# Down products of a feed-forward stage: one 128-row accumulation, or two 64-row accumulations in two PSUM banks

## Chip, cores and metric

The kernel runs on one core of a Trainium2 chip. The metric is device time in microseconds (us) of one execution of the program, the median of several. TensorE (PE in the profile, with its weight loads as PEld) multiplies, VectorE is DVE, ScalarE is ACT, GpSimd is POOL, SyncE is SP, and SP's DMA queue is SPq.

## What is computed

Two decoder layers over 288 token columns (256 of a prompt, 8 x 4 of samples). Each layer mixes by three branches (a recurrent one, windowed attention, pooling) and ends with the feed-forward part that the change touches:

```python
h = rmsnorm(x, norm_ffn) @ w_up                 # 1024 -> 4096
x = x + jnp.square(jax.nn.relu(h)) @ w_down     # 4096 -> 1024
```

All arrays are float32.

## The kernel before

**Layout.** Features lie on partitions, tokens along the free axis: `x` is 8 tiles of 128 x 288. Weights come in units of 128 x 1024 (eight 128 x 128 blocks) into a ring of four slots (`RING`), three units ahead (`LEAD`). Each unit is split into two reduced-precision halves: ACT copies it to `w_hi` (L720), DVE subtracts to get `w_lo` (L949). Activations are split likewise (`a_hi`, `a_lo` in front of the up products; `h_hi`, `h_lo` in front of the down products). A product of one 128 x 128 block is then three matmuls, hi x hi, hi x lo and lo x hi, each with a weight load of its own, so a unit is 8 x 3 = 24 matmuls of 128 rows, 128 output columns and 288 moving columns into one PSUM bank (`product`, L402). The four banks `PZ` take the units in turn. The four banks `PM` serve attention, norms and the recurrent state, and stand unused in the turns that the change touches.

**The feed-forward turns.** It is cut into `FI` = 4 turns of 16 units in each layer (`ffn_turn`, L671): units j = 0 to 7 are up products, each giving one of the eight tiles of h; units j = 8 to 15 are down products, each of which reads all eight tiles of h (k = 0 to 7) and gives one tile of x.

**Order of the work.** Each engine runs a list written by hand, and semaphores order the engines. In one turn, for an up unit, DVE waits for `unit_done`, takes relu times rstd out of PSUM (L1270), ACT squares it (L880) and copies it to `h_hi` (L882), DVE subtracts to get `h_lo` (L1274) and counts up `f_lo`. PE reads h with one wait for each k in unit 8 alone:

```python
have = (lambda k: pe.wait_ge(s["f_lo"], l * 8 * FI + i * 8 + (k + 1) + HEAD)) if j == 8 else None
product(out, u, lambda k: h_hi[:, k], lambda k: h_lo[:, k], KT, have)
```

For a down unit, DVE waits for `unit_done`, adds the bank to `x` (`add_to_x`, L992 to L994) and goes on to split a later unit. In the last turn of layer 0, DVE and ACT also make the next layer's `a_hi`, `a_lo` and sums of squares after each down unit, and after unit 15 DVE splits the next layer's first unit behind its addition to `x`. After the last unit of layer 1, the last tile of `x` is written out by a DMA.

**Other matmuls that the prediction uses.** `new_state` (L659 to L669) issues four matmuls with 32 rows each, from four groups of partitions, into four banks. The attention scores (L483 to L498) have 64 rows: first eight records of 128 columns on the lower 64 partitions, then eight on the upper 64, then some of 256 columns. A plain float32 matmul shows as two records, one of the split type as one.

Of the kernel before, what the change touches and what calls it, by code (L numbers as in the profile page):

```python
# [26 lines left out]
ALU = mybir.AluOpType  # L27
# [3 lines left out]
P = 128  # L31
DEPTH = 2
D_MODEL = 1024
KT = D_MODEL // P
# [4 lines left out]
T = NP + NS  # L39
# [15 lines left out]
HEAD = 1  # L55
# [6 lines left out]
U_FFN = 70  # L62
FI = 4
UNITS = U_FFN + FI * 16
RING = 4
# [5 lines left out]
T_BR, T_O, T_FFN = 50, 74, 82  # L71
# [90 lines left out]
def build(nc, io):  # L162
    _constants()
    ctx = ExitStack()
    with ctx:
        def sb(name, shape, dt=F32):
            return ctx.enter_context(nc.sbuf_tensor(name, shape, dt))
# [3 lines left out]
        w_hi = sb("w_hi", [P, RING, UW], F32R)  # L171
        w_lo = sb("w_lo", [P, RING, UW], F32R)
        x = sb("x", [P, KT, T])
        a_hi = sb("a_hi", [P, KT, T], F32R)
        a_lo = sb("a_lo", [P, KT, T], F32R)
        h_hi = sb("h_hi", [P, KT, T], F32R)
        h_lo = sb("h_lo", [P, KT, T], F32R)
# [13 lines left out]
        reg, at = {}, 0  # L191
# [74 lines left out]
        PM = [pm[:, i, :] for i in range(4)]  # L266
# [15 lines left out]
        s = Sems()  # L282
# [23 lines left out]
        def read_dve(l, t):  # L306

            return l * DVE_READS + (t + 1) + HEAD
# [89 lines left out]
        def _(pe):  # L398
# [3 lines left out]
            def product(outs, u, rhs_hi, rhs_lo, kk, have=None):  # L402

                for n, out in enumerate(outs):
                    for k in range(kk):
                        if have is not None and n == 0:
                            have(k)
                        hi = w_hi[:, u % RING].rearrange("p (k c) -> p k c", k=kk)[:, k, n * P:(n + 1) * P]
                        lo = w_lo[:, u % RING].rearrange("p (k c) -> p k c", k=kk)[:, k, n * P:(n + 1) * P]
                        mm(out, hi, rhs_hi(k), start=k == 0, stop=False)  # L410
                        mm(out, hi, rhs_lo(k), start=False, stop=False)
                        last = mm(out, lo, rhs_hi(k), start=False, stop=k == kk - 1)
                last.then_inc(s["unit_done"], 1)

            def unit(l, u):

                if l > 0 or u > 0:
                    pe.wait_ge(s["w_lo"], l * UNITS + (u + 1) + HEAD)
                if u < U_BR:
                    tiles = [u]  # L420
                elif u < U_O:
                    tiles = [T_BR + 2 * (u - U_BR), T_BR + 2 * (u - U_BR) + 1]
                else:
                    tiles = [T_O + u - U_O]
                for t4 in (t - 4 for t in tiles):
                    if t4 < 0:
                        pe.wait_ge(s["z_read_dve"], l * DVE_READS + HEAD)
                    else:
                        pe.wait_ge(s["z_read_dve"], read_dve(l, t4))
                outs = [PZ[t % 4][:, 0:T] for t in tiles]  # L430
                if u < U_BR:
                    def first_have(k):
                        pe.wait_ge(s["a_lo"], l * 16 + (k + 1))
                        if l == 0 and k % 4 == 0:
                            pe.sem_inc(s["pe_passed"], 1)
                            if k == 0:
                                pe.wait_ge(s["w0_lo"], 1)
                            else:
                                pe.wait_ge(s["w_lo"], 1 + HEAD)

                    product(outs, u, lambda k: a_hi[:, k], lambda k: a_lo[:, k], KT, first_have if u == 0 else None)
                elif u < U_O:
                    n, half = 2 - (u - U_BR) // 4, (u - U_BR) % 4
                    if half == 0:
                        if n == 2:
                            pe.wait_ge(s["oc_lo"], (l + 1) * G4)
                        elif n == 1:
                            pe.wait_ge(s["ob_lo"], (l + 1) * 4)
                        else:
                            pe.wait_ge(s["oa_lo"], l + 1 + HEAD)  # L450
                    hi, lo, o = ((a_hi, a_lo, 0), (h_hi, h_lo, 4), (h_hi, h_lo, 0))[n]
                    product(outs, u, lambda k: hi[:, o + k], lambda k: lo[:, o + k], 4)
                else:
                    have = (lambda k: pe.wait_ge(s["m_lo"], l * KT + (k + 1))) if u == U_O else None
                    product(outs, u, lambda k: h_hi[:, k], lambda k: h_lo[:, k], KT, have)

            def norm_sum(n):

                pe.wait_ge(s["consts_landed"], 16)
                pe.wait_ge(s["snew_read"], 8 * ((n - 1) // 2) + HEAD)  # L460
                pe.wait_ge(s["ssum"], n * KT + HEAD)
                mm(PM[3][:, 0:T], c("ones"), ssum).then_inc(s["nsum"], 1)
# [208 lines left out]
            def ffn_turn(l, i, first=False):  # L671
                for j in range(16):
                    u = U_FFN + j
                    pe.wait_ge(s["w_lo"], l * UNITS + i * 16 + (u + 1) + HEAD)
                    pe.wait_ge(s["z_read_dve"], i * 16 + read_dve(l, T_FFN + j - 4))
                    out = [PZ[(T_FFN + j) % 4][:, 0:T]]
                    if j < 8:
                        have = (lambda k: pe.wait_ge(s["a_lo"], l * 16 + (9 + k))) if first and j == 0 else None
                        product(out, u, lambda k: a_hi[:, k], lambda k: a_lo[:, k], KT, have)
                    else:  # L680
                        have = (lambda k: pe.wait_ge(s["f_lo"], l * 8 * FI + i * 8 + (k + 1) + HEAD)) if j == 8 else None
                        product(out, u, lambda k: h_hi[:, k], lambda k: h_lo[:, k], KT, have)
                    if first and j == 0:
                        norm_sum(2 * l + 2)
                    if first and j in (7, 12):
                        new_state(l, 0 if j == 7 else 4)
# [253 lines left out]
        def _(dve):  # L940
            chain = Chain(dve, "dve_chain", 0)
            tt, ts_, stt = nc.vector.tensor_tensor, nc.vector.tensor_scalar, nc.vector.scalar_tensor_tensor
            f = lambda a: a.bitcast(F32)

            def split(l, u, i=0):

                dve.wait_ge(s["w_hi"], l * UNITS + i * 16 + (u + 1))
                r = u % RING
                tt(w_lo[:, r], raw[:, r], f(w_hi[:, r]), ALU.subtract).then_inc(s["w_lo"], 1)  # L949
# [42 lines left out]
            def add_to_x(l, j, z, unit_done):  # L992
                dve.wait_ge(s["unit_done"], unit_done + HEAD)
                tt(x[:, j], x[:, j], z[:, 0:T], ALU.add).then_inc(s["z_read_dve"], 1)  # L994
# [268 lines left out]
            def mlp(l, i, last, first=False):  # L1263
                for j in range(16):
                    if j < 8:
                        dve.wait_ge(s["unit_done"], l * UNITS + i * 16 + (U_FFN + j + 1) + HEAD)
                        if first and j == 0:
                            dve.wait_ge(s["rstd"], 2 * l + 2)
                        dve.wait_ge(s["hsq"], l * 8 * FI + i * 8 + max(j - 1, 0) + HEAD)
                        stt(relu[:, j % 2], PZ[(T_FFN + j) % 4][:, 0:T], 0.0, rstd[:], ALU.max,  # L1270
                            ALU.mult).then_inc(s["z_read_dve"], 1)
                    for d in {0: (), 7: (6, 7)}.get(j, (j - 1,) if j < 8 else ()):
                        dve.wait_ge(s["f_hi"], l * 8 * FI + i * 8 + (d + 1))
                        tt(h_lo[:, d], hsq[:, d % 2], f(h_hi[:, d]), ALU.subtract).then_inc(s["f_lo"], 1)  # L1274
                    if j >= 8:
                        add_to_x(l, j - 8, PZ[(T_FFN + j) % 4], l * UNITS + i * 16 + (U_FFN + j + 1))
                        if first:
                            for q in {8: (0,), 9: (1,), 10: (2,), 11: (3,), 13: (4,), 14: (5,), 15: (6, 7)}.get(j, ()):
                                new_state(l, q)
                    if j + LEAD < 16 or not last:  # L1280
                        split(l, U_FFN + j + LEAD, i)
                    if last and j == 15 and l + 1 < DEPTH:
                        split(l + 1, 0)
                    if last and j >= 8 and l + 1 < DEPTH:
                        input_lo(2 * l + 3, j - 8, lambda k: pr(l, "norm_next", k))
                        add_square(2 * l + 3, j - 8)
                if last and l + 1 < DEPTH:
                    for u in range(1, LEAD):
                        split(l + 1, u)
# [37 lines left out]
            for j in range(KT):  # L1327
# [3 lines left out]
                if j in (0, 3):  # L1331
                    n = min(j, 1)
# [227 lines left out]
```

## Time and profile before

| what | value |
|---|---|
| median of 3 runs | 989.82 us (989.29 to 991.21) |
| the profiled execution's own time | 991.85 us |
| its span, first to last instruction | 990.0 us |
| mean granted TensorE clock | 0.995 |
| busy: PE / PEld / DVE / ACT / POOL | 961.6 / 927.9 / 671.6 / 489.2 / 38.2 us |
| matmul records | 8022 |

Durations below come from the profiled execution, which took 2.0 us more than the median; 1.85 us of its own time lie around the span. Matmuls are pipelined, so the duration of one in the trace is longer than the interval at which they follow each other; the interval is read from start to start. The granted clock is 1.00 at 2.4 GHz and 0.50 at 1.2 GHz.

### The profile page before, as it was taken

The page shows a single profiled execution, that of the slowest core. Times are in us where ns is not written, and L with a number is a line of the kernel's source. Part 1 is how long each engine was busy: PE and PEld are TensorE (multiplying, and loading weights), DVE is VectorE, ACT ScalarE, POOL GpSimd, SP SyncE. Part 2 cuts the span into 40 slices and gives each one's busy share as a digit, 9 for nine tenths or more (in the row PEclk, how much of TensorE's full clock was granted, in tenths as well). Part 3 has the DMA queues.
Part 4 walks back from the last instruction along what each step waited for, and adds up shares of the span by engine and source line. Part 5 has one row for each costly group of instructions (what it writes and reads, how often), then busy time and mean ns, then how long its engine had stood idle before and what let it go on. Part 6 is the DMA issues. An engine that isn't in the chain of part 4 may idle for free.

```text
span 990.0 us, 19113 instructions
## 1 busy us (share of the span) xinstructions
PE 961.6 (97%) x8022; PEld 927.9 (94%) x8022; DVE 671.6 (68%) x1051; ACT 489.2 (49%) x704; POOL 38.2 (4%) x60
## 2 busy tenths in 40 slices
PE   6999999989999999999999999989999999999998
PEld 5989898889999999999998999979899999999998
DVE  6678877866976765555656777778578767646463
ACT  6427662355466353445544295523745643535351
POOL 1050000000000000000000600000000000000000
PEclk9999999999999999999999999999999999999999
DMA  8543543333455485455373444434344545644542
GB/s 314 192 164 119 213 140 112 133 124 123 155 168 168 149 335 172 153 169 169 121 272 132 162 169 166 129 118 136 122 139 159 170 150 191 222 164 161 178 150 91
DMA packets 44021, 162.78 MB, mean 164 GB/s; under 512 B 5120, under 2 KB 6656, under 8 KB 43392
## 3 DMA queue, kind: packets, MB, share of 16 engines
q1 hardware_dynamic: 42512, 151.20, 45.2%
q0 software_dynamic: 1136, 9.83, 2.6%
q8 instruction: 64, 1.05, 0.4%
q10 hardware_dynamic: 288, 0.52, 0.2%
q14 instruction: 21, 0.17, 0.1%
HBM read 153.28 MB, written 10.29 MB: 165 GB/s over the span
## 4 chain that ended last, share of the span: by engine, by line
PE 88%; DVE 6%; issue 2%; ACT 1%; DMA 1%; SPq 0%; DVEq 0%; ACTq 0%
PE pz L400 80%; PE pm L400 8%; DVE w_lo L949 2%; ACT w_hi L720 1%; DMA raw<-in_w 1%; DVE arena L1168 1%; DVE arena L1169 1%; PE pm L526 1%; DVE arena L1230 1%; DVE h_lo L1261 0%; DVE arena L1249 0%; DVE arena L1216 0%; DVE arena L1153 0%; DVE arena L1152 0%; DVE arena L958 0%
## 5 line engine op out<-in xcount | busy, mean ns | idle before, releaser
L400 PE MATMUL pz<-a_hi,w_hi 128*128 128x288 f32 x1376 | 416.7, 303 | 10.8 <-DVE w_lo L1335 7.0
L400 PE MATMUL pz<-a_lo,w_hi 128*128 128x288 f32 x1376 | 408.5, 297 | 0.0
L400 PE MATMUL pz<-a_hi,w_lo 128*128 128x288 f32 x1376 | 407.1, 296 | 0.0
L720 ACT ACTIVATE w_hi<-raw 128x1024 fp32r<-128x1024 f32 x267 | 278.7, 1052 | 217.6 <-PE pz L400 214.3
L949 DVE TENSOR_TENSOR w_lo<-raw,w_hi 128x1024 fp32r<-128x1024 f32 x267 | 327.0, 1225 | 26.0 <-ACT w_hi L720 25.9
L400 PEld LDWEIGHTS pz<-a_hi,w_hi 128*128 128x128 f32 x1376 | 260.5, 189 | 19.0 <-DVE w_lo L1335 7.0
L400 PEld LDWEIGHTS pz<-a_lo,w_hi 128*128 128x128 f32 x1376 | 260.9, 190 | 1.1 <-issue 0.9
L400 PEld LDWEIGHTS pz<-a_hi,w_lo 128*128 128x128 f32 x1376 | 261.6, 190 | 0.0
L400 PE MATMUL pz<-h_hi,w_hi 128*128 128x288 f32 x768 | 228.5, 298 | 0.6 <-DVE h_lo L1261 0.6
L400 PE MATMUL pz<-h_lo,w_hi 128*128 128x288 f32 x768 | 226.6, 295 | 0.0
L400 PE MATMUL pz<-h_hi,w_lo 128*128 128x288 f32 x768 | 225.8, 294 | 0.0
L400 PEld LDWEIGHTS pz<-h_hi,w_hi 128*128 128x128 f32 x768 | 143.9, 187 | 4.4 <-issue 3.0
L400 PEld LDWEIGHTS pz<-h_hi,w_lo 128*128 128x128 f32 x768 | 144.6, 188 | 0.0
L400 PEld LDWEIGHTS pz<-h_lo,w_hi 128*128 128x128 f32 x768 | 144.2, 188 | 0.3
L994 DVE TENSOR_TENSOR x<-x,pz 128x288 f32<-128x288 f32 x80 | 36.3, 454 | 83.3 <-PE pz L400 81.9
L990 DVE TENSOR_TENSOR arena<-pz,rstd 128x288 f32<-128x288 f32 x92 | 41.5, 453 | 67.1 <-PE pz L400 64.5
L1270 DVE SCALAR_TENSOR_TENSOR arena<-pz,rstd 128x288 f32<-128x288 f32 x64 | 29.3, 458 | 78.3 <-PE pz L400 74.9
L400 PE MATMUL pm<-arena 128*32 128x16 f32 (+9 forms) x1400 | 60.2, 243 | 12.8 <-DVE arena L1169 6.1
L880 ACT ACTIVATE arena<-arena 128x288 f32<-128x288 f32 x64 | 28.4, 444 | 85.2 <-DVE arena L1270 85.2
L400 PEld LDWEIGHTS pm<-arena 128*32 128x32 f32 (+3 forms) x1400 | 42.1, 127 | 26.0 <-DVE arena L1169 8.5
L836 ACT ACTIVATE arena<-arena 128x1024 f32<-128x1024 f32 (+1 forms) x14 | 15.3, 1090 | 78.0 <-DVE arena L1153 78.0
L729 ACT ACTIVATE a_hi<-x,params 128x288 fp32r<-128x288 f32 x32 | 16.7, 534 | 32.4 <-DVE x L994 29.1
(169 smaller groups left out, 561.9 us busy)
## 6 DMA issues: line engine op xcount, KB each, us to landing
raw<-in_w SPq DMA_DIRECT2D x267, 512.0 KB, 3.4
arena<-in_s SPq DMA_DIRECT2D x2, 2048.0 KB, 9.4
out_ss_out<-arena POOLq DMA_DIRECT2D x2, 2048.0 KB, 8.1
out_u_out<-arena POOLq DMA_DIRECT2D x2, 864.0 KB, 7.5
arena<-in_kcT SPq DMA_DIRECT2D x2, 512.0 KB, 7.3
arena<-in_vc SPq DMA_DIRECT2D x2, 512.0 KB, 5.6
out_kc_out<-in_kc_kept POOLq DMA_DIRECT2D x1, 992.0 KB, 7.6
out_vc_out<-in_vc_kept POOLq DMA_DIRECT2D x1, 992.0 KB, 9.6
```

Source lines behind the costliest of these rows:

```text
L400: return nc.tensor.matmul(out, a, b, start=start, stop=stop, **kw)
L526: last = nc.tensor.transpose(PM[tg % 4][:, j * P:(j + 1) * P], src[j], c("ident"))
L720: act_fn(w_hi[:, r], raw[:, r], ACT.Copy).then_inc(s["w_hi"], 1)
L729: act_fn(a_hi[:, j], x[:, j], ACT.Copy, scale=weight(j)).then_inc(s["a_hi"], 1)
L836: act_fn(D[:, :, 0:w], D[:, :, 0:w], ACT.Exp).then_inc(s["level_e"], 1)
L880: act_fn(hsq[:, j % 2], relu[:, j % 2], ACT.Square).then_inc(s["hsq"], 1)
L949: tt(w_lo[:, r], raw[:, r], f(w_hi[:, r]), ALU.subtract).then_inc(s["w_lo"], 1)
L990: tt(out, z, rstd[:], ALU.mult).then_inc(s["z_read_dve"], 1)
L994: tt(x[:, j], x[:, j], z[:, 0:T], ALU.add).then_inc(s["z_read_dve"], 1)
L1168: tt(x0, level_views(KK, m)[0], d0, ALU.mult).then_inc(s["level_x"], 1)
L1169: tt(x1, level_views(ZQ, m)[1], d1, ALU.mult).then_inc(s["level_x"], 1)
L1270: stt(relu[:, j % 2], PZ[(T_FFN + j) % 4][:, 0:T], 0.0, rstd[:], ALU.max, ALU.mult).then_inc(s["z_read_dve"], 1)
```

## The change

In turns 1, 2 and 3 of each layer (i > 0), each down unit is computed as two accumulations, one over partitions 0 to 63 of every block and one over partitions 64 to 127. The lower halves accumulate in the unit's `PZ` bank, the upper halves in the `PM` bank of the same index; for each of the 24 block products the lower half is issued, then the upper half. So a unit has 48 matmuls of 64 rows. In front of each such unit PE waits until all eight tiles of `h_lo` are counted, in place of the waits for each k in unit 8. DVE adds the `PM` bank to `x`, waits for that addition, and then adds the `PZ` bank as before. Turn 0 of each layer and all up units are as they were.

```diff
+            def product_halves(outs, u):
+
+                for k in range(KT):
+                    at = slice(k * P, (k + 1) * P)
+                    for w, a in ((w_hi, h_hi), (w_hi, h_lo), (w_lo, h_hi)):
+                        for n, out in enumerate(outs):
+                            rows = slice(n * 64, (n + 1) * 64)
+                            last = mm(out, w[rows, u % RING, at], a[rows, k], start=k == 0 and w is w_hi and a is h_hi,
+                                      stop=k == KT - 1 and w is w_lo)
                 last.then_inc(s["unit_done"], 1)
...
                     else:
+                        if i > 0:
+                            pe.wait_ge(s["f_lo"], l * 8 * FI + i * 8 + 8 + HEAD)
+                            product_halves([out[0], PM[(T_FFN + j) % 4][:, 0:T]], u)
+                            continue
                         have = (lambda k: pe.wait_ge(s["f_lo"], l * 8 * FI + i * 8 + (k + 1) + HEAD)) if j == 8 else None
...
                     if j >= 8:
+                        if i > 0:
+                            dve.wait_ge(s["unit_done"], l * UNITS + i * 16 + (U_FFN + j + 1) + HEAD)
+                            tt(x[:, j - 8], x[:, j - 8], PM[(T_FFN + j) % 4][:, 0:T], ALU.add).then_inc(s["x_half"], 1)
+                            dve.wait_ge(s["x_half"], (l * (FI - 1) + i - 1) * 8 + j - 7)
                         add_to_x(l, j - 8, PZ[(T_FFN + j) % 4], l * UNITS + i * 16 + (U_FFN + j + 1))
```

## Rows read from the trace of the kernel before

**Rows 1.** The page's first part: busy us, share of span, instructions.

```profile
PE 961.6 (97%) x8022; PEld 927.9 (94%) x8022; DVE 671.6 (68%) x1051; ACT 489.2 (49%) x704; POOL 38.2 (4%) x60
```

**Rows 2.** The chain that ended last, by engine.

```profile
PE 88%; DVE 6%; issue 2%; ACT 1%; DMA 1%; SPq 0%; DVEq 0%; ACTq 0%
```

**Rows 3.** Turns 1 to 3 by stretch: engines' busy us, clock, DMA.

```profile
449.09:500.30 51.21, 51.21 (x386) 51.12 (x384) 31.81 (x52) 26.67 (x44) 0.00 (x0) 1.00 0.45 153
346.69:500.30 153.61, 153.61 (x1154) 153.53 (x1152) 90.71 (x140) 73.26 (x108) 1.52 (x3) 1.00 0.55 188
...
833.56:987.20 153.64, 153.64 (x1154) 153.53 (x1152) 85.18 (x126) 66.65 (x93) 0.54 (x1) 1.00 0.50 168
```

**Rows 4.** Timeline, PE, from unit 7 to unit 8 of a turn.

```profile
372.16 0.29 PE L400 MATMUL pz<-a_hi,w_lo 128*128 128x288 f32 x1
372.29 0.30 PE L400 MATMUL pz<-h_hi,w_hi 128*128 128x288 f32 x1
```

**Rows 5.** Timeline, DVE, at the same place.

```profile
372.49 0.46 DVE L1270 SCALAR_TENSOR_TENSOR arena<-pz,rstd 128x288 f32<-128x288 f32 x1 [1.24 <-PE pz L400]
...
373.94 0.46 DVE L1274 TENSOR_TENSOR h_lo<-arena,h_hi 128x288 fp32r<-128x288 f32 x1 [0.62 <-ACT h_hi L882]
```

**Rows 6.** Timeline, layer boundary: DVE's split, then PE's first matmuls.

```profile
500.86 1.22 DVE L949 TENSOR_TENSOR w_lo<-raw,w_hi 128x1024 fp32r<-128x1024 f32 x1
...
502.13 0.40 PE L400 MATMUL pz<-a_hi,w_hi 128*128 128x288 f32 x1 [1.68 <-DVE w_lo L949]
502.37 0.29 PE L400 MATMUL pz<-a_lo,w_hi 128*128 128x288 f32 x1
```

**Rows 7.** Timeline, PE, 64-row matmuls and the 128-row ones behind them.

```profile
69.14 1.99 PE L400 MATMUL pm<-arena 64*128 64x256 f32 x8
71.06 0.40 PE L400 MATMUL pz<-a_hi,w_hi 128*128 128x288 f32 x1
71.30 0.29 PE L400 MATMUL pz<-a_lo,w_hi 128*128 128x288 f32 x1
```

**Rows 8.** Timeline, DVE, the last addition to x.

```profile
987.36 0.45 DVE L994 TENSOR_TENSOR x<-x,pz 128x288 f32<-128x288 f32 x1 [2.74 <-PE pz L400]
```

**Rows 9.** Timeline, four 32-row matmuls from four partition groups.

```profile
318.65 0.20 PEld L400 LDWEIGHTS pm<-arena 32*128 32x128 f32 x4 [0.17 <-issue]
...
318.65 0.71 PE L400 MATMUL pm<-arena 32*128 32x512 f32 x4
```

**Rows 10.** Groups by form: the same matmuls, busy us, mean ns of one.

```profile
L400 PE MATMUL pm<-arena 32*128 32x512 f32 x32 | 4.6, 640 | 0.0
```

**Rows 11.** Stretches of the 64-row scores: PE and PEld, with counts.

```profile
59.53:60.03 0.50, 0.50 (x5) 0.50 (x5) 1.00 0.00 0
60.08:60.53 0.45, 0.45 (x10) 0.45 (x9) 1.00 0.00 0
```

**Rows 12.** Timeline, PE, a stretch at granted clock 0.50.

```profile
24.37 0.45 PE L400 MATMUL pz<-a_lo,w_hi 128*128 128x288 f32 x1
24.61 0.45 PE L400 MATMUL pz<-a_hi,w_lo 128*128 128x288 f32 x1
```

**Rows 13.** Timeline, PE, a burst of small matmuls.

```profile
178.68 0.74 PE L400 MATMUL pm<-arena 128*32 128x16 f32 x64
```

**Rows 14.** Timeline, PE, behind the longest idle stretch before 30 us.

```profile
22.73 0.41 PE L400 MATMUL pz<-a_hi,w_hi 128*128 128x288 f32 x1 [1.84 <-DVE w_lo L949]
```

**Rows 15.** Stretches around idle TensorE: busy us, then clock, DMA share, GB/s.

```profile
23.00:26.40 3.40, 3.40 (x16) 3.40 (x16) 3.04 (x5) 1.01 (x2) 0.00 (x0) 0.50 0.75 260
...
157.00:160.00 3.00, 0.62 (x22) 0.48 (x24) 3.00 (x7) 0.00 (x0) 0.59 (x1) 0.92 0.54 208
160.00:163.00 3.00, 3.00 (x68) 2.83 (x59) 2.32 (x3) 0.64 (x1) 0.00 (x0) 0.51 0.25 82
...
500.00:503.00 3.00, 1.32 (x10) 1.08 (x9) 2.51 (x5) 2.02 (x4) 0.00 (x0) 1.00 0.00 0
503.00:506.00 3.00, 3.00 (x23) 2.90 (x22) 2.19 (x2) 1.70 (x2) 0.00 (x0) 1.00 0.97 345
```

More of the change, by code:

```diff
@@ L413, in product @@
                 last.then_inc(s["unit_done"], 1)
+            def product_halves(outs, u):
[6 more added lines that the diff above has]
+                                      stop=k == KT - 1 and w is w_lo)
+                last.then_inc(s["unit_done"], 1)
             def unit(l, u):
```

## The prediction

> **What bounds the kernel now.** I read the page's first part, then the chain that ended last, then the feed-forward turns by stretch, then single places. PE is busy 961.6 us of a 990.0 us span [rows 1] and holds 88% of the chain [rows 2]: what PE gains or loses is nearly all of the time. The changed turns 1 to 3 show it without a gap: 153.61 us in layer 0 and 153.64 in layer 1, PE busy in all of it, for 1152 weight loads each [rows 3]. So a matmul follows the last one after 153.6/1152 = 133.3 ns, a unit of 24 takes 3.20 us, and from unit 7 to unit 8 of a turn there is no step either (372.16 to 372.29 [rows 4]). In the last turn of layer 0 DVE, with the most to do there, works 31.8 of 51.2 us and ACT 26.7 [rows 3]. The question is what PE does with twice as many matmuls of half the rows, and what it newly waits for.
>
> **Step 1: the wait in front of unit 8.** Before, unit 8 started at 372.29 and came to the eighth tile of h only in its last eighth. Now it waits for all eight. The last of them is late: DVE takes unit 7 out of PSUM at 372.49, ACT squares and copies, and DVE's last `h_lo` runs from 373.94 for 0.46, to 374.40 [rows 5]. PE starts some 0.05 us after such a release (split over at 500.86 + 1.22 = 502.08, matmul recorded at 502.13), and its first matmul stands idle for its weights: the second follows 0.24 us behind, not 0.13, so 0.11 more [rows 6]. The first matmul thus runs from 374.40 + 0.05 + 0.11 = 374.56 in place of 372.29: 2.27 us. Nothing stands behind PE that could fill it (up units of the next turn come later in its list), and DVE and ACT do the same in that chain as before. Six turns: **13.6 us**. The units behind unit 8 find the count reached. Splits and DMAs for later units get more time by it.
>
> **Step 2: from 64 rows back to 128.** Eight 64-row records begin at 69.14 and end at 71.13. In the full-row stream the next matmul starts 0.29 - 0.13 = 0.16 us before the last one ends, which would be 70.97; the next ones here start at 71.06 and 71.30, so the first ran from 71.30 - 0.13 = 71.17 [rows 7]. That is 0.20 us a time. It is paid where a divided turn is followed by a full-row unit without a gap: after turns 1 and 2 of each layer, 4 x 0.20 = **0.8 us**. After turn 3 of layer 0 it hides in the gap of step 4, after that of layer 1 nothing follows. The way into 64 rows lies within step 1's wait; without that cover it would be as much again, 1.2 us.
>
> **Step 3: the pairs.** 48 units x 24 = 1152 pairs of 64-row matmuls replace 1152 matmuls of 128 rows. Side by side a pair takes 133.3 ns and the step costs nothing; one after the other 266.7 ns and 153.6 us. No row shows this pair at this type. The nearest are four 32-row matmuls from four partition groups into four banks: four loads are over in 0.20 us and four matmuls in 0.71 [rows 9], where one takes 0.64 on average [rows 10]. So they ran together. The 64-row scores show the same: in 0.50 us with the lower partitions alone 5 matmuls and 5 loads are in flight, in 0.45 us where the upper ones join them 10 and 9 [rows 11]. I take 133.3 ns and **0 us**. Both ends stay in the range: at 1.2 GHz the interval is 24.61 - 24.37 = 0.240 us [rows 12], of which half is 120 ns, so at 2.4 GHz 13.3 ns stand on top of the columns, and no row says of what. If halves shed them, the step gives 1152 x 13.3 = 15.4 us back; if the second load adds them once more, it costs 15.4. Four instructions in 133 ns are no issue limit: 64 matmuls, each with its load, went in 0.74 us [rows 13].
>
> A row and a rule stand against each other here. Loads of four groups overlap almost wholly [rows 9], so two half loads cost one. The Trainium skill (TensorE: Matmul & The Clock Gate, Part 2, on LDWEIGHTS) says that a load takes as long for few rows as for 128, since only its columns count. By that rule alone, with loads in file, a pair would be bound by two loads. Rows 9 decide for overlap at 32 rows; the rule is the second rival below.
>
> **Step 4: DVE's additions.** Each divided unit gets one more addition of 0.45 us [rows 8] and the wait for it, which I take at 0.05 like the release of step 1. Eight more in the last turn of layer 0 bring DVE from 31.8 to some 36 us of 51.2 [rows 3]; behind the waiting DVE stands the split of a unit three ahead, over 6 us early. So it costs nothing there. It costs 0.5 us at two places: at the layer boundary, where DVE adds, then splits the next layer's first unit while PE stands (1.68 us today [rows 6]), and at the end, where the last addition at 987.36 [rows 8] precedes the last output DMA. **1.0 us.**
>
> **Step 5: the clock.** Steps 1 and 4 leave PE idle seven times: six times from 372.16 + 0.29 = 372.45 to 374.45, 2.0 us, and at the boundary for 1.68 + 0.5 = 2.2. What such a gap does today is mixed. After 1.84 us [rows 14] the granted clock went to 0.50, 1.2 GHz, until 26.4 [rows 15]. In 157 to 160, with PE busy only 0.62 us, it fell too (0.92, then 0.51 [rows 15]). After the 1.68 us at the boundary it stayed at 1.00 [rows 15]. Low stretches held 3.4 us. At 240 ns a matmul [rows 12] one holds 14.2 matmuls in place of 25.5: 11.3 x 133.3 ns = 1.5 us lost. The new gaps are a little longer than the 1.84 and the 1.68, so I take four falls of seven, **6.0 us**, with 0 and 7 x 1.5 = 10.5 as ends.
>
> **Sum.** 13.6 + 0.8 + 0 + 1.0 + 6.0 = 21.4 us. On the profiled execution the span goes from 990.0 to 1011.4 and its own time from 991.85 to 1013.3. That execution lies 2.0 us above the median; on the median, 989.82 + 21.4 = 1011.2, so **1011 us**.
>
> **Rivals.**
>
> *Halves are faster, and pay for the wait.* If a pair takes 120 ns, step 3 gives 15.4 back, against 13.6 + 0.8 + 1.0 = 15.4 of steps 1, 2 and 4: 989.8 us without a fall of the clock, 995.8 with four. It is no slower only if the pair is at 120 ns or under and the clock never falls. For it: the 13.3 ns are unexplained. Against: eight 64-row records of 256 columns take 1.99 us [rows 7], that is nothing less than two clocks a column (213 ns) each; half the rows bought nothing there. 12%, two of them down to no change.
>
> *Loads in file.* Load to load is 0.11 us where PE waits for one (step 1's 0.11); two in file make 0.21 to 0.22, above the 133.3, and a pair costs 81 ns more: 1152 x 81 ns = 93 us, 1104 us. For it: no row has two 64-row loads for 288-column matmuls of the split type. Against: rows 9 and 11. 3%.
>
> *Streams overlap in part.* Two halves write two banks at full rate, where the rows that I lean on had plain float32 at half of it. From 138 to 174 ns a pair, the time is 1017 to 1058 us. For it: four took 0.71 against 0.64 [rows 9, 10]. Against: that excess is the exposed first load. The Trainium skill (TensorE: Matmul & The Clock Gate, Part 3, measured speedups) gives 3.07 times for four row tiles, not 4. An estimate from that page: a pair 1.30 times as long, 40 ns x 1152 = 46 us, 1057 us. 14%, of which 10 up to 150 ns.
>
> *The change doesn't do what it says.* Halves run one after the other: 989.8 + 15.4 + 153.6 = 1159 us. Against: rows 9 and 11. 3%.
>
> **How the numbers follow.** My forecast, pairs at 133 ns with zero to seven falls, is 1005 to 1016 us: 68%. The range 1000 to 1027 adds pairs down to 129 ns (upper part of the first rival, 4%) and up to 147 ns (1011 + 15.4; 9%): 81%. Below it lies the rest of the first rival, above it the others. A measurement of this kernel tells about 0.2%, 2 us, from no change. Faster by more than that needs a pair under 118 ns: 2%. Within: 2%. Slower: 96%.
>
> **What would show it.** A step of about 2.3 us between units 7 and 8 in six turns, PE waiting for DVE L1274's line; the matmuls of a divided unit still at 3.20 us a unit, two in flight at each start; 0.2 us more at the ends of turns 1 and 2; the boundary's wait at 2.2 us in place of 1.68; a mean granted clock a little below 0.995, with 0.50 behind some of the gaps. I am wrong if a divided unit takes clearly more or less than 3.20 us, which counts 48-fold, or if the clock falls at each gap or at none.

## The result, and the profile after

| what | before | after |
|---|---|---|
| median of 4 runs each | 989.56 us (988.93 to 991.21) | 1012.23 us (1010.1 to 1014.03) |
| the profiled execution's span / own time | 990.0 / 991.85 us | 1012.2 / 1014.03 us |
| mean granted TensorE clock | 0.995 | 0.987 |

The ratio is 1.0226, 95% interval 1.0202 to 1.0249: 22.7 us slower, where 21.4 were forecast.

The page's first part and the chain by engine, to set against [rows 1, 2]. PE has 1152 more records, yet only 9.6 us more busy time, and in these lies what the lower clock costs behind the new gaps. The other 12.6 us of the longer span are idle time of PE.

```profile
PE 971.2 (96%) x9174; PEld 935.0 (92%) x9174; DVE 693.4 (69%) x1099; ACT 488.8 (48%) x704; POOL 39.3 (4%) x60
...
PE 87%; DVE 7%; issue 2%; ACT 2%; DMA 1%; SPq 0%; DVEq 0%; ACTq 0%
```

The waits of PE on DVE (us in total, times, longest). The first row is new: six waits, one for each changed turn, all on the last `h_lo` (L1289 here, L1274 before). The second is that at the layer boundary.

```profile
PE pz L400 <- DVE h_lo L1289: 12.5, 6, 2.1
...
PE pz L400 <- DVE w_lo L964: 3.0, 2, 2.2
```

The timeline where turn 1 of layer 0 goes from unit 7 to unit 8 [rows 4, 5]. The last matmul of unit 7 begins at 371.50. DVE takes that unit out of PSUM at 371.84 (relu, L1285), the last `h_lo` follows at 373.27, and only then the first pair starts, both halves at 373.88. PE stood for 2.08 us; before, the step was 0.13 us. It starts 0.15 us after the last `h_lo` is done (373.27 + 0.46 = 373.73). The next lower half comes 0.24 us later, the interval of 1.2 GHz [rows 12].

```profile
371.50 0.29 PE L400 MATMUL pz<-a_hi,w_lo 128*128 128x288 f32 x1
371.84 0.46 DVE L1285 SCALAR_TENSOR_TENSOR arena<-pz,rstd 128x288 f32<-128x288 f32 x1 [1.24 <-PE pz L400]
...
373.27 0.46 DVE L1289 TENSOR_TENSOR h_lo<-arena,h_hi 128x288 fp32r<-128x288 f32 x1 [0.62 <-ACT h_hi L897]
...
373.88 0.44 PE L400 MATMUL pz<-h_hi,w_hi 64*128 64x288 f32 x1 [2.08 <-DVE h_lo L1289]
...
373.88 0.50 PE L400 MATMUL pm<-h_hi,w_hi 64*128 64x288 f32 x1
...
374.12 0.44 PE L400 MATMUL pz<-h_lo,w_hi 64*128 64x288 f32 x1
```

The granted clock behind the seven gaps (six in front of unit 8, at 512 that of the layer boundary), and at the first also in the stretch that follows (same columns as [rows 3], the clock third from the end). It is 0.50 to 0.56 behind the gaps at 374, 483, 872, 927 and 982, and 1.00 behind those at 429 and 512. At 377 to 380 it is 0.93: it had come back.

```profile
374.00:377.00 3.00, 3.00 (x26) 3.00 (x28) 0.87 (x1) 0.19 (x1) 0.00 (x0) 0.51 0.26 74
377.00:380.00 3.00, 3.00 (x46) 3.00 (x44) 1.07 (x3) 1.05 (x1) 0.00 (x0) 0.93 0.28 109
429.00:432.00 3.00, 2.88 (x43) 2.91 (x45) 1.11 (x1) 0.43 (x1) 0.00 (x0) 1.00 0.29 51
483.00:486.00 3.00, 3.00 (x28) 3.00 (x30) 0.84 (x1) 0.16 (x1) 0.00 (x0) 0.54 0.33 93
512.00:515.00 3.00, 2.61 (x19) 2.61 (x20) 3.00 (x5) 2.94 (x4) 0.00 (x0) 1.00 0.48 143
872.00:875.00 3.00, 3.00 (x32) 3.00 (x31) 0.30 (x1) 0.00 (x0) 0.00 (x0) 0.56 0.54 149
927.00:930.00 3.00, 3.00 (x30) 3.00 (x28) 0.53 (x1) 0.00 (x0) 0.00 (x0) 0.50 0.44 119
982.00:985.00 3.00, 3.00 (x26) 3.00 (x28) 0.79 (x1) 0.11 (x1) 0.00 (x0) 0.50 0.33 81
```

The timeline of pairs at full clock, weight loads (PEld) too. Lower half to lower half is 0.13 us (400.27 to 400.40), the upper half is 0.03 us behind its lower half, and the two loads run beside each other as well (400.27 and 400.30, 0.18 each).

```profile
400.26 0.29 PE L400 MATMUL pz<-h_hi,w_hi 64*128 64x288 f32 x1
400.27 0.18 PEld L400 LDWEIGHTS pz<-h_lo,w_hi 64*128 64x128 f32 x1
400.29 0.29 PE L400 MATMUL pm<-h_hi,w_hi 64*128 64x288 f32 x1
400.30 0.18 PEld L400 LDWEIGHTS pm<-h_lo,w_hi 64*128 64x128 f32 x1
400.40 0.29 PE L400 MATMUL pz<-h_lo,w_hi 64*128 64x288 f32 x1
400.40 0.19 PEld L400 LDWEIGHTS pz<-h_hi,w_lo 64*128 64x128 f32 x1
400.43 0.29 PE L400 MATMUL pm<-h_lo,w_hi 64*128 64x288 f32 x1
```

The groups by form, weight loads (busy us, mean ns of one): a load takes 192 ns for 64 rows and 189 for 128.

```profile
L400 PEld LDWEIGHTS pz<-a_hi,w_hi 128*128 128x128 f32 x1376 | 259.9, 189 | 18.5 <-DVE w_lo L1354 7.0
...
L400 PEld LDWEIGHTS pm<-h_hi,w_hi 64*128 64x128 f32 x384 | 73.9, 192 | 0.0
```

DVE beside them: the new addition (L1293) and the old one (L1009, was L994) for each unit, 3.20 us from one unit to the next, as PE's pairs say.

```profile
398.09 0.45 DVE L1293 TENSOR_TENSOR x<-x,pm 128x288 f32<-128x288 f32 x1 [1.12 <-PE pm L400]
398.58 0.46 DVE L1009 TENSOR_TENSOR x<-x,pz 128x288 f32<-128x288 f32 x1
398.95 1.22 DVE L964 TENSOR_TENSOR w_lo<-raw,w_hi 128x1024 fp32r<-128x1024 f32 x1
401.29 0.45 DVE L1293 TENSOR_TENSOR x<-x,pm 128x288 f32<-128x288 f32 x1 [1.12 <-PE pm L400]
```

The layer boundary and the end [rows 6, 8]. The new addition stands ahead of the old one and of the split, 0.49 us from start to start, and PE's wait is 2.17 us in place of 1.68.

```profile
510.25 0.45 DVE L1293 TENSOR_TENSOR x<-x,pm 128x288 f32<-128x288 f32 x1 [0.77 <-PE pm L400]
510.74 0.45 DVE L1009 TENSOR_TENSOR x<-x,pz 128x288 f32<-128x288 f32 x1
511.12 1.22 DVE L964 TENSOR_TENSOR w_lo<-raw,w_hi 128x1024 fp32r<-128x1024 f32 x1
...
512.39 0.40 PE L400 MATMUL pz<-a_hi,w_hi 128*128 128x288 f32 x1 [2.17 <-DVE w_lo L964]
...
1009.12 0.45 DVE L1293 TENSOR_TENSOR x<-x,pm 128x288 f32<-128x288 f32 x1 [2.25 <-PE pm L400]
1009.61 0.45 DVE L1009 TENSOR_TENSOR x<-x,pz 128x288 f32<-128x288 f32 x1
```

The way back to 128 rows, at the end of turn 1 of layer 0. The first full-row matmul starts 0.22 us after the last half and shows its load (0.40 in place of 0.29), and the second follows 0.24 us later.

```profile
400.96 0.29 PE L400 MATMUL pm<-h_hi,w_lo 64*128 64x288 f32 x1
401.18 0.40 PE L400 MATMUL pz<-a_hi,w_hi 128*128 128x288 f32 x1
401.42 0.30 PE L400 MATMUL pz<-a_lo,w_hi 128*128 128x288 f32 x1
```

**Where the 22.2 us of span went.** Read from the last matmul of one unit to that of the next, the six changed turns took 55.06, 53.73 and 55.24 us in layer 0 and 55.05, 55.25 and 55.15 in layer 1, against 51.20 each: 22.3 us more. Of a turn, unit 8 took 5.54 us at 429, where the clock stayed up, and 6.97 to 7.07 where it fell, against 3.20. So the wait costs 2.34 us (six times, 14.1 together), and a fall of the clock 1.43 to 1.53 more (five times, 7.5 together). The other seven down units took 22.40 together, 3.20 each; the eight up units behind a divided turn took 25.78 in place of 25.60 (0.183 more, four times). The boundary's unit took 5.63 against 5.14, and the stretch from the start of the last matmul to the end 3.44 against 2.95. That is 23.3 us; the rest of the kernel was 1.1 us shorter in this execution. Stretches at 0.50 number eight after (27.3 us) and three before (10.2 us).

### The profile page after: what moved, and what is told of

Read it like the earlier page. It is cut to its first block, busy times and chain, and to the rows that moved or that the text cites. A ratio compares the mean times of both kernels' runs of the same rounds, so it can differ in the third digit from the quotient of the medians.

```text
span 1012.2 us, 21513 instructions
## 1 busy us (share of the span) xinstructions
PE 971.2 (96%) x9174; PEld 935.0 (92%) x9174; DVE 693.4 (69%) x1099; ACT 488.8 (48%) x704; POOL 39.3 (4%) x60
## 4 chain that ended last, share of the span: by engine, by line
PE 87%; DVE 7%; issue 2%; ACT 2%; DMA 1%; SPq 0%; DVEq 0%; ACTq 0%
PE pz L400 75%; PE pm L400 11%; DVE w_lo L964 2%; ACT w_hi L735 1%; DMA raw<-in_w 1%; DVE arena L1183 1%; DVE arena L1184 1%; PE pm L537 1%; DVE arena L1245 0%; DVE h_lo L1276 0%; DVE h_lo L1289 0%; DVE arena L1285 0%; DVE arena L1264 0%; DVE arena L1005 0%; ACT arena L895 0%
## 5 line engine op out<-in xcount | busy, mean ns | idle before, releaser
L400 PE MATMUL pz<-h_hi,w_hi 128*128 128x288 f32 (+1 forms) x768 | 231.1, 301 | 13.1 <-DVE h_lo L1289 12.5
L400 PE MATMUL pz<-h_lo,w_hi 128*128 128x288 f32 (+1 forms) x768 | 228.8, 298 | 0.0
L400 PE MATMUL pz<-h_hi,w_lo 128*128 128x288 f32 (+1 forms) x768 | 228.0, 297 | 0.0
L400 PEld LDWEIGHTS pz<-h_hi,w_hi 128*128 128x128 f32 (+1 forms) x768 | 145.8, 190 | 18.1 <-issue 16.8
L400 PEld LDWEIGHTS pz<-h_hi,w_lo 128*128 128x128 f32 (+1 forms) x768 | 146.7, 191 | 0.0
L400 PEld LDWEIGHTS pz<-h_lo,w_hi 128*128 128x128 f32 (+1 forms) x768 | 146.2, 190 | 0.3
L400 PE MATMUL pm<-h_hi,w_hi 64*128 64x288 f32 x384 | 116.4, 303 | 0.0
L400 PE MATMUL pm<-h_lo,w_hi 64*128 64x288 f32 x384 | 115.5, 301 | 0.0
L400 PE MATMUL pm<-h_hi,w_lo 64*128 64x288 f32 x384 | 115.1, 300 | 0.0
L1285 DVE SCALAR_TENSOR_TENSOR arena<-pz,rstd 128x288 f32<-128x288 f32 x64 | 29.2, 457 | 76.2 <-PE pz L400 72.8
L400 PEld LDWEIGHTS pm<-h_hi,w_lo 64*128 64x128 f32 x384 | 74.3, 193 | 0.0
```

Of the source, the lines that this page charges most:

```text
L400: return nc.tensor.matmul(out, a, b, start=start, stop=stop, **kw)
```

## The experiments

The theory: the wait for all eight tiles stands in front of unit 8 and starts most falls of the clock; the division itself costs nothing but the turns in and out of 64 rows and two additions. The rivals are in the expectations. e1, e2, e3, e5, e10 and e11 were timed several times each, beside the kernel before; e4, e7, e8, e9, e12 and e13 are one run each.

**e1_wait_per_k.** The divided units, with the wait for each tile as before.

```diff
-            def product_halves(outs, u):
+            def product_halves(outs, u, have=None):
                 for k in range(KT):
+                    if have is not None:
+                        have(k)
...
-                            pe.wait_ge(s["f_lo"], l * 8 * FI + i * 8 + 8 + HEAD)
-                            product_halves([out[0], PM[(T_FFN + j) % 4][:, 0:T]], u)
+                            have = (lambda k: pe.wait_ge(s["f_lo"], l * 8 * FI + i * 8 + (k + 1) + HEAD)) if j == 8 else None
+                            product_halves([out[0], PM[(T_FFN + j) % 4][:, 0:T]], u, have)
```

> The divided units stay, but unit 8 of a divided turn waits for each tile of h_lo as it comes to it, as before the change. My account (a wait of 2.27 us in six turns, and the clock falls that it brings; pairs cost nothing): what is left is the way into and out of 64 rows, (6 + 4) x 0.2 us, the later additions, 1.0 us, and at most one fall of the clock at the layer boundary, 1.5 us, so 992.6 to 994.1 us, with no idle time of PE in front of unit 8 over 0.3 us. Rival, the pairs or DVE's additions are what costs: the time stays within a few us of 1012.

Measured: 993.08 us against 990.01, ratio 1.0029 (1.0017 to 1.0041). The mean clock is 0.997, unit 8 takes 3.38 us, the others 3.20, the way back costs 0.19, the boundary's unit 5.63. PE's only wait for `h_lo` that is left is one of 0.3 us, twice, in the undivided turns. So 19.6 of the 22.7 us were the wait and what it did to the clock. What stays is 3.1 us, inside the span expected, and the trace sums it to 2.8: 6 x 0.18 into and 4 x 0.19 out of 64 rows, and 2 x 0.49 of additions.

**e2_wait_alone.** The kernel before, undivided, with the wait for all eight tiles.

```diff
                     else:
+                        if i > 0:
+                            pe.wait_ge(s["f_lo"], l * 8 * FI + i * 8 + 8 + HEAD)
                         have = (lambda k: pe.wait_ge(s["f_lo"], l * 8 * FI + i * 8 + (k + 1) + HEAD)) if j == 8 else None
```

> The kernel before, its matmuls undivided, with the one wait for all eight tiles of h_lo put in front of unit 8 in turns 1 to 3. My account: 6 x 2.27 = 13.6 us for the wait and 1.5 us for each fall of the clock in six gaps of 2.0 us, none to six, so 1003 to 1012 us, most likely near 1009. Rival, the wait is not what costs: within 2 us of 989.6.

Measured: 1012.61 us, ratio 1.0226 (1.0203 to 1.0248), 0.6 us above the upper end of the span given, where all six falls would lie. PE's waits:

```profile
PE pz L400 <- DVE h_lo L1276: 13.2, 6, 2.2
```

A gap is 13.2/6 = 2.20 us, 0.12 longer than the 12.5/6 = 2.08 of the changed kernel. PE starts 0.26 us after the last `h_lo` here and 0.15 there; why was not tried. Unit 8 takes 5.62 us without a fall and 7.15 with one; four of six fell in the profiled run, where the six turns took 20.6 us more, 14.5 for the waits (6 x 2.42) and 6.1 for the falls. A wait without any division costs as much as the change. The two parts, 3.1 us in e1 and 22.6 here, add up to 3.0 more than the 22.7 of the change. Of these 3.0 the way into 64 rows, which the wait covers, is 6 x 0.18 = 1.1 and the shorter unit 8 is 6 x 0.08 = 0.5; the rest is inside the intervals.

**e3_filled.** The changed kernel, with 15 matmuls that nothing uses in front of the wait.

```diff
                         if i > 0:
+                            if j == 8:
+                                for _ in range(15):
+                                    mm(PM[0][:, 0:T], w_hi[:, u % RING, 0:P], a_hi[:, 0])
                             pe.wait_ge(s["f_lo"], l * 8 * FI + i * 8 + 8 + HEAD)
```

> The changed kernel, with 15 more full-row matmuls of 288 columns in front of the wait of unit 8 in each divided turn, into a PSUM bank that is free then; their result is not used. They fill the 2.0 us in which PE stood idle. My account: the wait is as long as before (13.6 us), but the clock stays at 1.00 there, so the time falls by the falls of the clock alone, 1.5 us each, to 1005 us, or 1006.5 with one fall at the layer boundary; mean granted clock about 0.995. Rival, the clock was not part of it: 1012 us, as the wait itself is not shorter.

Measured: 1003.39 us, ratio 1.0134 (1.0109 to 1.0159). One stretch at 0.50 is left in the whole run, and unit 8 with its fill takes 5.46 us in every turn, 2.26 more than 3.20: the 15 matmuls take as long as the wait did. So PE is nearly as late as with the gap, and the time is 8.8 us less (1012.23 - 1003.39), 1.6 below the 1005 expected. The five falls at the gaps are 7.5 us in the trace of the changed kernel. The 8.8 us hold low stretches at other places too, one here against three there.

**e4_in_file, e7_in_file_no_gap, e13_in_file_filled.** All 24 lower halves of a unit, then all 24 upper ones; e4 keeps the wait for all tiles, e7 has the waits for each k, e13 is e4 with e3's fill.

```diff
-                for k in range(KT):
-                    at = slice(k * P, (k + 1) * P)
-                    for w, a in ((w_hi, h_hi), (w_hi, h_lo), (w_lo, h_hi)):
-                        for n, out in enumerate(outs):
-                            rows = slice(n * 64, (n + 1) * 64)
+                for n, out in enumerate(outs):
+                    rows = slice(n * 64, (n + 1) * 64)
+                    for k in range(KT):
+                        at = slice(k * P, (k + 1) * P)
+                        for w, a in ((w_hi, h_hi), (w_hi, h_lo), (w_lo, h_hi)):
```

> The changed kernel, with the same 48 half-row matmuls a unit, but all 24 lower halves first and then all 24 upper halves. If two halves run together only because they are issued in turn: 24 x 133 ns more in each of 48 units, 153.6 us, so 1166 us. If TensorE finds them in whatever order they are issued: 1012 us. Between them: it looks ahead only a few matmuls.

Measured for e4: 1338.07 us at a mean clock of 0.812: a miss by 172 us. The windows show a turn's divided units, and the first unit of 128 rows behind it:

```profile
374.00:450.00 76.00, 76.00 (x368) 76.00 (x367) 14.31 (x21) 7.40 (x7) 0.00 (x0) 0.50 0.18 56
...
454.00:457.00 3.00, 3.00 (x21) 3.00 (x21) 0.41 (x2) 0.00 (x0) 0.00 (x0) 0.87 0.55 175
457.00:460.00 3.00, 3.00 (x25) 3.00 (x24) 1.39 (x3) 1.84 (x3) 0.00 (x0) 1.00 0.27 31
```

PE is busy in all 76 us and the clock is 0.50 throughout; it comes back only in the next turn's first unit. The six turns are alike: six low stretches of 79 to 85 us each. The timeline at a change of half shows how far the halves overlap: three or four matmuls of each interleave, the rest go in file at 0.24 us.

```profile
400.83 0.44 PE L400 MATMUL pm<-h_lo,w_hi 64*128 64x288 f32 x1
401.07 0.44 PE L400 MATMUL pm<-h_hi,w_lo 64*128 64x288 f32 x1
401.08 0.60 PE L400 MATMUL pz<-h_hi,w_hi 64*128 64x288 f32 x1
401.31 0.44 PE L400 MATMUL pm<-h_hi,w_hi 64*128 64x288 f32 x1
401.48 0.44 PE L400 MATMUL pz<-h_lo,w_hi 64*128 64x288 f32 x1
401.55 0.44 PE L400 MATMUL pm<-h_lo,w_hi 64*128 64x288 f32 x1
401.72 0.44 PE L400 MATMUL pz<-h_hi,w_lo 64*128 64x288 f32 x1
401.79 0.44 PE L400 MATMUL pm<-h_hi,w_lo 64*128 64x288 f32 x1
401.96 0.44 PE L400 MATMUL pz<-h_hi,w_hi 64*128 64x288 f32 x1
402.20 0.44 PE L400 MATMUL pz<-h_lo,w_hi 64*128 64x288 f32 x1
```

Each change of half also shows matmuls that start out of the order in which they were issued: the lower half of the next unit starts at 401.08, ahead of three upper ones of the unit before (401.31, 401.55, 401.79).

The theory that came out of it, that half rows at work bring the clock down by themselves, went into e7, with the rival that only the gap does.

> The halves in file again (24 lower, then 24 upper), but with the waits for each tile of h_lo, so that no idle stretch of 2 us precedes them. In the first such kernel the clock was at 0.50 through the divided units. If matmuls on half of the rows alone are enough for that: again 0.50 there, and about 12 us less than its 1338, near 1325. Rival, it was the idle stretch that brought the clock down: 1.00 in the divided units, and with the overlap of some three matmuls that the trace of the first one shows at each change of halves (20.7 intervals a half in place of 24), 993 + 48 x 0.73 x 3.2 = 1105 us.

Measured for e7: 1107.95 us at 0.994. The theory falls, the rival holds: the same order of half rows, with no gap in front, runs at 1.00.

```profile
374.00:410.00 36.00, 36.00 (x314) 36.00 (x314) 12.60 (x19) 6.63 (x7) 0.00 (x0) 1.00 0.32 104
```

e7 differs from e4 in its waits too, so e13 keeps e4's wait and fills the gap:

> The halves in file by 24, with the wait for all tiles, as in the run that took 1338 us, but with 15 full-row matmuls in front of the wait so that PE does not stand idle; their result is not used. If a clock that has come down stays down while only half of the rows work at a time, and one that is up stays up, then without the idle stretch it is at 1.00 in the divided units and the time is that of the run in file without a gap plus the wait, 1108 + 13 = 1121 us. If half of the rows bring it down by themselves behind such a wait: near 1330 us.

Measured for e13: 1120.43 us, and again a clock of 1.00, 5.54 us a unit as in e7.

```profile
376.00:419.00 43.00, 43.00 (x368) 42.83 (x368) 15.81 (x24) 8.48 (x8) 0.00 (x0) 1.00 0.28 91
```

So e4's clock did not come down without the idle gap, and it was not raised again while one half worked at a time.

**e8_threes, e12_sixes, e9_twelves.** e1 with the halves alternating by 3, 6 and 12 matmuls in place of 1 (the group is 1, 2 or 4 blocks; here 4).

```diff
-                for k in range(KT):
...
+                for k0 in range(0, KT, 4):
+                    for n, out in enumerate(outs):
+                        rows = slice(n * 64, (n + 1) * 64)
+                        for k in range(k0, k0 + 4):
...
```

> As the kernel with waits for each tile, but the halves alternate in groups of three matmuls (one block: three lower, three upper) and not one by one. In the kernel with the halves in file, the first upper matmul started while three lower ones were still to come. If TensorE looks ahead by that much, three in file still run beside the other three: 993 us, 3.2 us a unit, clock as before. Rival, only neighbours pair: three in file, then three, 993 + 153.6 = 1147 us, or near 1325 if the clock falls as well.

> The same in groups of six. With a look-ahead of 3.2 matmuls 2 x (6 - 3.2) = 5.6 intervals for six are less than six, so each half can run through: 3.2 us a unit and 993 us, with the upper halves some three matmuls behind. If it were below three: 48 x 24 x 133 ns x (1 - 2.5/3) = 26 us or more on top.

> As the kernel with waits for each tile, the halves alternating in groups of twelve matmuls. In file by 24, a unit took 5.54 us without an idle stretch ahead, 41.6 intervals of 133.3 ns for 2 x 24: some 3.2 matmuls overlap at each change of halves. If the look-ahead is that and no more: 2 x (12 - 3.2) = 17.6 intervals for twelve, 4.7 us a unit, 993 + 48 x 1.5 = 1065 us, clock at 1.00. Rival, the tile units take whatever comes within a unit: 993 us.

Measured: 992.61, 997.28 and 1066.4 us; a unit takes 3.20, 3.20 and 4.68 us, and 5.54 by 24 (e7). Of the 48 matmuls of a unit, 3.2 are hidden at each change of half. That gives (48 - 2 x 3.2) x 133.3 ns = 5.55 us by 24 and (48 - 4 x 3.2) x 133.3 = 4.69 by 12. The 3.2 was read off the first of these, so only the second tests it. By 6, eight changes would hide 25.6, more than the 24 of a half, and a half is hidden whole. e12 missed its 993: its unit 8 takes 3.77 us, 0.38 more than one by one (6 x 0.38 = 2.3 us), as six lower matmuls less the 3.2, 2.8 intervals, run alone at its start. The rest goes with low clock at other places of that one run, whose mean was 0.993.

**e10_one_unit.** e1, with unit 8 alone divided in each of the six turns.

```diff
-                        if i > 0:
+                        if i > 0 and j == 8:
...
-                            dve.wait_ge(s["x_half"], (l * (FI - 1) + i - 1) * 8 + j - 7)
+                            dve.wait_ge(s["x_half"], l * (FI - 1) + i)
```

> As the kernel with waits for each tile, but only the first down unit (j = 8) of turns 1 to 3 is divided, six units in place of 48; the other seven run with full rows. That kernel was 3.1 us over the one before. My account: the way into 64 rows and back is paid six times each, 12 x 0.2 = 2.4 us, and no addition falls on the layer boundary or the end, so 2.4 us over the kernel before. Rival, the 3.1 us lie in the pairs themselves (2.7 ns each over 1152 of them): an eighth of it is left, 0.4 us over the kernel before.

Measured: 991.24 us against 990.71, ratio 1.0012 (0.9999 to 1.0025). The time, 1.2 us more, lies between the two and can't tell. The trace can: each of the six turns takes 51.57 us, 0.37 more (0.18 in, 0.19 out), 2.2 us together. So the rival, that the pairs themselves cost, does not hold. Going in and out costs as much for one divided unit as for eight.

**e5_split_first, e11_boundary.** The kernel before. In e5 DVE makes the next layer's first split ahead of the last addition to x. In e11 ACT and DVE make the splits of its first two units behind j = 14 and 15, and PE asks for one read of the banks less in front of that layer's first unit.

```diff
+                    if last and j == 15 and l + 1 < DEPTH:
+                        split(l + 1, 0)
                     if j >= 8:
...
-                    if last and j == 15 and l + 1 < DEPTH:
-                        split(l + 1, 0)
```

```diff
-                        pe.wait_ge(s["z_read_dve"], l * DVE_READS + HEAD)
+                        pe.wait_ge(s["z_read_dve"], l * DVE_READS + HEAD - (1 if l > 0 and t4 == -4 else 0))
...
-                    if last and j == 15 and l + 1 < DEPTH:
-                        split(l + 1, 0)
+                    if last and j >= 14 and l + 1 < DEPTH:
+                        split(l + 1, j - 14)
...
```

> The kernel before, undivided, with one step moved: at the last unit of layer 0, DVE splits the next layer's first unit ahead of the addition of that unit to x, not behind it. My account of the layer boundary (the split behind the addition is what PE stands 1.68 us for): the wait goes, the next layer's second unit waits some 0.5 us for its own split in its place, so 1.2 us less than the kernel before, 988.4 to 988.8. Rival, PE waits for something else there (the last tile of a_lo): no change that can be measured.

> The kernel before, undivided, mended at the layer boundary: ACT and DVE split the next layer's first unit behind unit 14 of the last turn and its second unit behind unit 15, ahead of the last tile's activations, and PE's first unit no longer waits for the last addition to x, which reads another bank. Before, that unit ended 5.14 us after the last one where 3.20 us are its matmuls. If the split is the cause: 3.2 to 3.4 us, so 1.8 us less than the kernel before; more than the 0.83 us that the trace of the kernel with one split moved shows at this place (5.14 to 4.31). Rival, the last tile of a_lo then holds PE for as long: no more than 0.8 us less.

Measured: e5 988.35 us against 990.71, ratio 0.9982 (0.9966 to 0.9997), the boundary's unit 4.31 us in place of 5.14, 0.8 less where 1.2 were expected; e11 987.26 against 989.58, ratio 0.9976 (0.9962 to 0.9989), its unit 3.56, where 3.2 to 3.4 were expected, 1.6 less than before. The boundary's DVE list is on the path, as Step 4 had it. In e11's timeline PE goes over the boundary with no gap, 499.31 to 499.44:

```profile
499.31 0.29 PE L400 MATMUL pz<-h_hi,w_lo 128*128 128x288 f32 x1
499.44 0.30 PE L400 MATMUL pz<-a_hi,w_hi 128*128 128x288 f32 x1
```

e11 is faster than both kernels, 2.3 us under the one before, and divides nothing.

## Why the prediction was right

The forecast's mechanism held, and so did every term but one to within 0.5 us; the number of falls of the clock was too small by one.

**Step 1** (2.27 us a turn, 13.6): 2.34 at 429, where the clock stayed up, so 14.1. PE starts 0.15 us after the last `h_lo`, not the 0.05 taken, and the second pair comes 0.03 sooner than taken. e2 shows that the wait does it without any division.

**Step 2** (0.20 us a time, 0.8): 0.183 in the changed kernel, 4 x 0.183 = 0.7. The way in, which was said to lie within Step 1's wait, costs 0.18 once that cover is gone (e1, e10). The Trainium skill (TensorEngine Tiling (Array Packing), Key Properties) says that a change of the tiling mode drains TensorE. e10 agrees in that each change costs, 0.18 and 0.19 us a time; no run here shows that it is a drain.

**Step 3** (133.3 ns a pair, 0): 3.20 us a unit, so nothing to two decimals. The first rival needed pairs at 120 ns: refuted. Loads in file needed 0.21 to 0.22 us, refuted: two loads start 0.03 us apart. A partial overlap needed 138 ns or more: refuted. The Trainium skill (TensorE: Matmul & The Clock Gate, Part 2, on LDWEIGHTS) says that a load takes as long for few rows as for 128. The trace agrees, 192 ns for 64 rows and 189 for 128. What the rival took from it, that the loads of two halves follow each other, did not come. The Trainium skill (same page, Part 3) gives 3.07 times for four row tiles, from which the prediction worked out its estimate of 1057 us. Here two row tiles lost nothing. The last rival, halves one after the other (1159 us), did not come either; e7 issues them so, and even then a part overlaps: 1107.95.

**Step 4** (0.5 us at two places, 1.0): 0.49 and 0.49. Beside the running units the additions cost nothing.

**Step 5** (four falls of seven at 1.5 us, 6.0) is the term that was mis-sized: five fell in the profiled run, 7.5 us. The price of one was right, 1.43 to 1.53. The number was a choice between rows that pointed both ways, and zero to seven lay within the forecast, so that the sum came within 1.3 us of the median's rise is in part luck. The mean granted clock of the four runs goes from 0.987 (1014.03 us) to 0.990 (1010.1 us), so the number of low stretches differs from run to run.

With these, 14.1 + 0.7 + 0 + 1.0 + 7.5 = 23.3 us, and the rest of the kernel 1.1 shorter, the span's 22.2 are told.

What stays open is when such a gap brings the clock down. A gap of 2.1 us did so at the entry of five turns and not at 429. The boundary's 2.17 us did not in the changed kernel, nor in e1 and e3, but it did in e7, e8, e9, e12 and e13. So the length of the gap alone does not decide it. The lines are those behind the boundary in e8 and in e12:

```profile
504.00:505.00 1.00, 1.00 (x6) 1.00 (x5) 0.77 (x1) 0.28 (x1) 0.00 (x0) 0.50 1.00 398
...
503.00:504.00 1.00, 1.00 (x6) 1.00 (x6) 1.00 (x2) 1.00 (x3) 0.00 (x0) 0.50 0.32 61
```

It also stays open what the 13.3 ns are that a matmul takes beyond its columns; halves did not shed them.

## What to carry to other kernels

A wait for the whole of an input in front of the first consumer costs the producer's latency, 2.34 us here, each time; a wait for each piece hides it, even where the division behind it is kept (e1). When PE is the bound, price a new gap twice: its own length, and 1.5 us for each fall of the clock that may follow. Two row halves cost nothing by themselves when they alternate closely (by 1 to 3 matmuls here), but they buy nothing for full 128-row operands, and each way in and out and each addition on the path is paid on top.

## What the runs showed that was not expected

**The clock kept its level while one half worked at a time.** Down by the gap, it stayed at 0.50 through the eight divided units of a turn with PE busy all the time (e4); up, it stayed at 1.00 in the same order of matmuls (e7, e13). With both halves together it came back within the next stretch (0.51, then 0.93 in the changed kernel). In e7 and e13 it fell at the boundary, right behind such units, and the low stretch there lasted 6.8 us, against 3.4 behind the same gap in e8, e9 and e12. Why was not tried.

**PE overlaps two halves only about three matmuls deep.** By 24 and by 12, each change of half hid 3.2 matmuls (5.54 and 4.68 us a unit). Alternating by 1, 3 and 6 gives 3.20 us, a half hidden whole. These are one run each, but for e1.

**A single divided unit pays the whole toll**: 0.37 us for the way in and out (e10), as much as eight.
